# Hybrid decoder trunk on one core: in the norm behind a feed-forward, the third weight unit is split after the second tile, and TensorE takes three units side by side in the first token half

## The reference

```python
for i in range(2):
    h = modulate(x, norm_g[i, 0], shift, scale)              # rmsnorm(x, g) * (1 + scale) + shift
    x = x + 0.5 * gate * swiglu(h, ffn_w13[i, 0], ffn_w2[i, 0])
    h = modulate(x, norm_g[i, 1], shift, scale)
    x = x + gate * (mlstm_mixer(h, ...) if i == 0 else diff_attn_mixer(h, ...))
    h = modulate(x, norm_g[i, 2], shift, scale)
    x = x + 0.5 * gate * swiglu(h, ffn_w13[i, 1], ffn_w2[i, 1])
return rmsnorm(x, final_g)
```

## Time and profile before

| | us |
|---|---|
| median of 3 runs | 1873.6 (1873.27 to 1873.88) |
| span of the profiled execution | 1871.5 |
| median less that span | 2.1 |
| PE busy | 1853.9 (99%) |
| DVE busy | 1476.3 (79%) |
| ACT busy | 900.7 (48%) |

### The profile page before, as it was taken

How to read it: one execution, slowest core, us unless ns; L and a number is a source line. 1 busy time by engine, 2 the same in 40 slices (tenths; PEclk the granted TensorE clock), 3 DMA queues, 4 the chain that set the end, 5 groups by cost and what they waited for, 6 DMA issues and landing times. The chain is left out here.

```text
span 1871.5 us, 30964 instructions
## 1 busy us (share of the span) xinstructions
PE 1853.9 (99%) x12020; PEld 1683.2 (90%) x12020; DVE 1476.3 (79%) x2078; ACT 900.7 (48%) x1438; POOL 31.9 (2%) x29
## 2 busy tenths in 40 slices
PE   8999999999999999999999999999999999999998
PEld 6999988888779999998899999889877799999887
DVE  7999978795679988868688887896787798888433
ACT  6566532344335756642255655224444556656322
POOL 5000000000000000000010000000000000000000
PEclk9999999999999999999999999999999999999999
DMA  8344369634115232359643232972321232332432
GB/s 326 127 147 168 118 251 333 219 92 156 57 46 192 68 112 90 112 212 340 212 152 105 104 112 87 349 248 82 113 68 46 92 133 91 113 104 92 139 98 84
DMA packets 84115, 270.86 MB, mean 145 GB/s; under 512 B 8593, under 2 KB 16913, under 8 KB 83258
## 3 DMA queue, kind: packets, MB, share of 16 engines
q1 hardware_dynamic: 83616, 267.62, 41.4%
q0 software_dynamic: 352, 2.11, 0.3%
q10 hardware_dynamic: 58, 0.00, 0.0%
HBM read 261.30 MB, written 8.40 MB: 144 GB/s over the span
## 5 line engine op out<-in xcount | busy, mean ns | idle before, releaser
L2095 DVE TENSOR_TENSOR w_lo<-arena,w_hi 128x1024 fp32r<-128x1024 f32 (+1 forms) x288 | 307.6, 1089 | 93.7 <-ACT w_hi L1375 90.8
L1293 ACT ACTIVATE w_hi<-arena 128x640 fp32r<-128x640 f32 (+1 forms) x214 | 192.2, 899 | 357.4 <-DMA arena<-w 177.9
L729 PE MATMUL acc<-h_hi,w_hi 128*128 128x256 f32 (+1 forms) x1130 | 357.4, 316 | 3.1 <-DVE h_lo L2701 1.4
L731 PE MATMUL acc<-h_hi,w_lo 128*128 128x256 f32 (+1 forms) x1130 | 348.5, 308 | 0.0
L730 PE MATMUL acc<-h_lo,w_hi 128*128 128x256 f32 (+1 forms) x1130 | 348.5, 308 | 0.0
L1838 DVE TENSOR_TENSOR w_lo<-arena,w_hi 128x768 fp32r<-128x768 f32 (+1 forms) x211 | 215.0, 1021 | 139.7 <-ACT w_hi L1293 138.2
L1375 ACT ACTIVATE w_hi<-arena 128x1024 fp32r<-128x1024 f32 (+1 forms) x288 | 273.4, 950 | 70.9 <-PE stats L731 30.7
L729 PE MATMUL outp<-g_hi,w_hi 128*128 128x512 f32 (+1 forms) x792 | 290.3, 367 | 0.0
L730 PE MATMUL outp<-g_lo,w_hi 128*128 128x512 f32 (+1 forms) x792 | 289.5, 365 | 0.0
L731 PE MATMUL outp<-g_hi,w_lo 128*128 128x512 f32 (+1 forms) x792 | 289.4, 365 | 0.0
L729 PEld LDWEIGHTS acc<-h_hi,w_hi 128*128 128x128 f32 x1130 | 215.6, 191 | 20.4 <-issue 2.9
(11 more groups left out here) (338 smaller groups left out, 3656.0 us busy)
## 6 DMA issues: line engine op xcount, KB each, us to landing
arena<-w SPq DMA_DIRECT2D x166, 512.0 KB, 4.4
arena<-ada SPq DMA_DIRECT2D x58, 512.0 KB, 5.7
ada_raw<-ada SPq DMA_DIRECT2D x57, 512.0 KB, 5.6
arena<-w SPq DMA_DIRECT2D x64, 384.0 KB, 3.5
arena<-w SPq DMA_DIRECT2D x64, 320.0 KB, 4.2
arena<-wa SPq DMA_DIRECT2D x33, 512.0 KB, 3.5
arena<-wb SPq DMA_DIRECT2D x32, 512.0 KB, 3.5
early_ada<-ada SPq DMA_DIRECT2D x8, 1024.0 KB, 17.5
```

The source lines that it names most:

```text
L729: pe.matmul(bank, a_hi, b_hi, start=start, stop=False, skip_group_check=onto)
L731: return pe.matmul(bank, a_lo, b_hi, start=False, stop=stop, skip_group_check=onto)
L1293: act.activation(dst[:, 0:n], src[:, 0:n], ACT.Copy).then_inc(hi_ready, 1)
L2095: dve.tensor_tensor(slot(w_lo[s], n), two_factors(p, j, n), slot(w_hi[s], n).bitcast(F32), ALU.subtract)\
```

## The change

It touches norms 1, 3 and 4 alone. ACT makes the high part of unit U + 2 behind `split_high` of k = 1 instead of k = 4. DVE makes the low part of U + 2 behind `mod` 3 and ahead of `h_lo` 2, instead of behind `h_lo` 7. TensorE does k = 0 and k = 1 of half 0 with two units as before; at k = 2 it waits for the third unit after the two units' products and makes up its k = 0, 1 and 2; from k = 3 to 7 three units go side by side. `norm_sum(n, 1)` moves behind k = 6. Unit U + 3 then follows alone.

```diff
                 for half in range(2):
-                    together = 3 if half else 2
+                    third = half == 0 and n in (1, 3, 4)
+                    together = 3 if half or third else 2
                     side_by_side = KT - 2 if half else KT
                     for k in range(side_by_side):
                         pe.wait_ge(act_lo_ready, Q_IN[n] + 8 * half + k + 1)
-                        for s in range(together):
-                            if half == 0 and k == 0:
+                        for s in range(2 if third and k < 2 else together):
+                            if half == 0 and (k == 0 or third and k == 2 and s == 2):
                                 pe.wait_ge(lo_ready, U + s + 1)
                                 take_acc(T, s)
+                            if third and k == 2 and s == 2:
+                                product(s, 0, half)
+                                product(s, 1, half)
                             product(s, k, half)
+                        if third and k == KT - 2:
+                            norm_sum(n, 1)
...
                     split_high(Q_IN[n] + k, k, tok(0), ada_v[:, 3 * n, :])
-                    if k == 4:
+                    if k == (4 if mixer else 1):
                         high_part(U + 2)
...
-            def lows(q, bias, make, t=slice(0, S)):
+            def lows(q, bias, make, t=slice(0, S), ahead_of_third=lambda: None):
...
                         make(k)
+                    if k == 3:
+                        ahead_of_third()
                     if k >= 1:
                         low(k - 1)
...
-                lows(Q_IN[n], ada_v[:, 3 * n, :], lambda k: modulated(k, 0), tok(0))
-                low_part(U + 2)
+                def third_unit():
+                    if not mixer:
+                        low_part(U + 2)
+
+                lows(Q_IN[n], ada_v[:, 3 * n, :], lambda k: modulated(k, 0), tok(0), third_unit)
+                if mixer:
+                    low_part(U + 2)
```

## The result

The changed kernel takes 1880.77 us (median of 5 runs, 1878.98 to 1881.52), the kernel before 1873.81: a ratio of 1.0037, 95% interval 1.0027 to 1.0048. It is slower by 7.0 us where 4.9 were forecast. The profiled execution took 1878.98 us, with a span of 1877.2, 5.7 more than the 1871.5 of before.

The account below looks back on a forecast made before the run. PE, 99% busy and paced by DVE within a norm, bounds the kernel. Stops 7.34 - 3.48 won back + 0.30 restarts + 0.72 ahead of half 1 = 4.88 us; span 1876.4, median 1878.5, range 1874.8 to 1882.0.

Parts of the forecast that it names:

- One of the signs that the prediction named: In the trace after, the granted clock was to stay at 1.00 through TensorE's late start of k = 2.
- The stop at k = 2: TensorE idle before k = 2, waiting on transfer and DVE's low part: 2.37, 2.46, 2.51 us, 7.34 in all.
- The constants from elsewhere in the trace: Transfer issue to ACT's start 3.55; ACT's high part plus signal 1.09; DVE's low part 1.14; `h_lo` to TensorE's start 0.54 us.
- -1.16: TensorE's standing still per norm between k = 2 and half 1 before the change, all to be won back: 1.16 us.
- the restart: Slow first matmul behind a stop on TensorE, 0.39 instead of 0.28 us: 0.10 us per stop.
- The small stop ahead of half 1: TensorE, with fewer products to cover sum to first tile, stops 0.14 us plus 0.10 restart: 0.24 per norm.
- rival 3: Clock falls in the k = 2 stop, 2.4 to 1.2 GHz: 1.2 us per norm, 1882.2, or 1897 if lasting; 7%.
- rival 4: Third unit's transfer lands after 4.4 us, so the three stops grow by 0.9, 0.8 and 0.9 us: 1881.1; 5%.
- The rival of a load that is in time: Third unit in by 370.36, leaving DVE's 1.14 us as only price: 1 us in all, 1874.6; 17% with half-way cases.
- The gain: TensorE finds both halves of the third unit with `h_lo` 2 in time: 2.8 us faster, 1870.8; 5% with other faster cases.

Follow-up runs that it names:

- Experiment 4: Changed kernel, with a buffer of its own for the third unit so its transfer need not wait for the low part of U: 1874.14 us, ratio 1.0005.
- experiment 5: Changed kernel with only ACT's and DVE's orders moved, TensorE's order as before the change: 1880.17 us, ratio 1.0039.
- experiment 6: Changed kernel with only TensorE's order moved, ACT's and DVE's orders as before the change: 1890.05 us, ratio 1.0088.
- second trace: Trace of the changed kernel run once more with no edit: 1880.74 us, ratio 1.0038 to the kernel before.
- experiment 2: Changed kernel with 18 thrown-away matmuls ahead of TensorE's wait for k = 2 in norms 1, 3 and 4: 1879.04 us, ratio 1.0030.
- experiment 3: Changed kernel with 9 thrown-away matmuls ahead of TensorE's wait for k = 2 in norms 1, 3 and 4: 1878.52 us, ratio 1.0025.
- experiment 8: Kernel before, with own third-unit buffer, its high part behind k = 0, low part on GpSimd, TensorE three units from k = 3, second sum behind k = 4: 1880.61 us.

## Why the prediction was right, and where it was short

**The place and the mechanism.** The forecast of slower, by ACT waiting for the transfer with the splits queued behind it and by DVE's low part ahead of `h_lo` 2, holds step by step. Experiment 4 takes the first half away, experiments 5 and 6 show whose order makes the stop. One of the signs that the prediction named did not come: the granted clock was not at 1.00 throughout.

**The stop at k = 2.** Forecast 2.37, 2.46 and 2.51 us; measured 2.38, 2.33 and 2.49 (norm 3: 939.95 to 943.08 is 3.13, less the 0.80 of before; norm 4: 1292.54 to 1295.82 is 3.28, less 0.79 or 0.80). The constants from elsewhere in the trace (3.55 from issue to ACT's start, 1.09, 1.14, 0.54) carried over to within 0.03 in norms 1 and 4. The 0.13 in norm 3 is the transfer: 3.65 was assumed from the issue to ACT's start, and it took 3.51 (936.80 to 940.31).

**What comes back and what is lost again.** The forecast had -1.16 + 0.10 + 0.24 = -0.82 per norm. Its last 0.10, the restart, lies behind the first matmul of half 1, so up to that matmul it is -0.92; measured is 1.45 - 2.38 = -0.93 in norm 1 and 1.57 - 2.49 = -0.92 in norm 4. The small stop ahead of half 1 is there: the first matmul of half 1 starts 0.27 us after the one ahead instead of 0.12, forecast 0.14 later. Norms 1 and 4 and the second trace's norm 3, which had no fall, add 1.45 + 1.57 + 1.39 = 4.4 us up to half 1. With the three restarts behind it that is 4.7, against the 4.88 of the forecast.

**The term that was mis-sized.** It is rival 3, the clock. It was given 7% as a case of its own, and stood in the sum of 4.88 as nothing; it is in both traces of the changed kernel, and 8 of its 10 times lie above all 17 of experiments 2 and 3. Its price was near (1.2 us per norm assumed, 1.4 to 1.6 measured), its chance was not, and a price that may come on top of the forecast should have been a term with an expected number of falls, not a rival to it. That is why the median is 1880.8 where 1878.5 was said: the forecast's stops came nearly to the tenth, the time was 2.3 us off. By the time alone rival 4 (1881.1, slower transfers) would have fitted best; the three transfers, with 3.56, 3.51 and 3.53 us from issue to ACT's start, rule it out. The argument against it, that the work on both sides of the stop is dense, fell: dense work on both sides did not keep the clock. The rule of the Trainium skill named in the prediction ("TensorE: Matmul & The Clock Gate", "HAM oscillation — how this bites in real kernels") describes matmul bursts that wait for a transfer and find the clock throttled in every tile. The traces agree in kind, and differ in degree: in the page's example each wait of about 3 to 5 us has a slow start behind it, here the waits are shorter, 1.9 to 2.4 us, and each trace shows a slow start behind one in three. The measurement decides.

**The rival of a load that is in time** has its price from experiment 4, +0.96 us against the 1.0 that was worked out. **The gain** was not seen in any version with three units side by side.

**Not separated.** How many norms fall in a run without a trace; what decides in which norm the clock falls; the 1.1 us of experiment 2 ahead of norm 5; the 1.3 us by which the openings differ between traces, the 0.6 us from norm 1 to norm 3 and the 0.9 us behind norm 4.

## What to carry to other kernels

Before a conversion of a loaded unit (here its high part) is moved forward in an engine's queue, look when its input's transfer is issued, not only whether it was in time at the old place: what stood behind the instruction waits with it, and here six tiles of every norm did. When one engine paces another, a step moved ahead on the pacing engine costs its full length at once (1.14 us), and wider work on the paced engine can only win back the stops that were there before (1.16 us); do this sum first. And a new stop on TensorE has a second price behind it, the clock: stops of 1.9 to 2.4 us were followed by the lower level in some norms (1.4 to 1.6 us each in the changed kernel), those of 4.4 us in all three, those of 1.0 to 1.2 us in none of six.

## What the runs showed of the hardware

- The clock fell behind idle stretches of 1.9 to 2.4 us between dense work in one of three norms in each of four traces (changed kernel twice, experiments 5 and 8), not always the same norm, and each time for about 3.3 us of slow matmuls (0.21 us from start to start instead of 0.12). With 1.0 to 1.2 us idle (experiments 3 and 4) it fell in none of six norms; with 4.4 us (experiment 6) in three of three.
- GpSimd's `tensor_tensor` with two inputs in SBUF held DVE's `scalar_tensor_tensor` with two inputs in SBUF for its whole length (2.59 us instead of 0.47). The Trainium skill ("SBUF — State Buffer", section "SBUF: two separate sides") has the rule: the port pair that the two engines share is an exclusive lock, held for the whole instruction, and a DVE instruction with two SBUF inputs needs it. The traces agree with it: in the opening of the kernel before, DVE's `tensor_tensor` with two inputs in SBUF was held too (1.73 us for 512 columns, against 1.2 for 1024), while `stats` (0.76 us) and `h_lo` (0.75 us), which have one input in PSUM, lie wholly under GpSimd instructions and are no longer for it.
